# Merge stage of an encoder block: how the inverse row sums of the attention are read, and which engine issues the reads

## The reference, cut to what matters

```python
probs = p / (jnp.sum(p, axis=-1, keepdims=True) + jnp.exp(sink - m))      # branch A; branch B: softmax
ya = swa_gqa_sinks(...) @ w_o_a[l];  yb = chunk_relbias_attention(...) @ w_o_b[l]
gates = jax.nn.sigmoid(h @ w_branch_gate[l] + b_branch_gate[l]).reshape(b, s, N_BRANCHES, d)
mixed = gates[:, :, 0] * ya + gates[:, :, 1] * yb
x = x + mixed @ w_out[l]
h2 = rmsnorm(x, norm_ffn[l])
g_logits = jnp.dot(hf, w_rg) + b_rg;  e_logits = jnp.dot(hf, w_re) + b_re
```

## Time and profile before

| what | us |
|---|---|
| three timed runs | 2922.29, 2931.5, 2965.14 |
| their median | 2931.5 |
| the profiled execution, its own time | 2918.7 |
| its span, first to last instruction | 2917.1 |
| mean granted TensorE clock | 0.915 of full speed |
| TensorE busy with matmuls | 2510.5 (86% of the span) |
| VectorE, ScalarE, GpSimd busy | 1341.9, 1045.2, 702.0 |

### The profile page before, as it was taken

How to read it: one execution, slowest core, us unless ns; L and a number is a source line. 1 busy time by engine, 2 the same in 40 slices (tenths; PEclk the granted TensorE clock), 3 DMA queues, 4 the chain that set the end, 5 groups by cost and what they waited for, 6 DMA issues and landing times. The chain is left out here.

```text
span 2917.1 us, 37013 instructions
## 1 busy us (share of the span) xinstructions
PE 2510.5 (86%) x12254; PEld 2071.1 (71%) x12255; DVE 1341.9 (46%) x1962; ACT 1045.2 (36%) x1705; POOL 702.0 (24%) x693
## 2 busy tenths in 40 slices
PE   3899986899996999959389999947999999999950
PEld 3788865788884777748288888836888888888840
DVE  7101122100003666626433332256876767787958
ACT  4111111111113566624321111114654646666722
POOL 4264555500000000000022112102332323233342
PEclk9999998999996999959699998968999999999975
DMA  4245566761214544165553433336886868798968
GB/s 138 87 135 168 202 186 182 226 242 65 86 50 125 125 118 97 43 139 127 168 158 126 137 124 113 101 118 246 315 303 230 316 230 316 260 373 316 352 231 330
DMA packets 237631, 540.18 MB, mean 185 GB/s; under 512 B 55840, under 2 KB 90080, under 8 KB 232304
## 3 DMA queue, kind: packets, MB, share of 16 engines
q1 hardware_dynamic: 190160, 400.73, 41.7%
q0 software_dynamic: 27056, 89.67, 9.3%
q10 hardware_dynamic: 20336, 48.77, 4.6%
HBM read 405.07 MB, written 134.02 MB: 185 GB/s over the span
## 5 line engine op out<-in xcount | busy, mean ns | idle before, releaser
L394 DVE TENSOR_TENSOR pj_w_lo<-pj_w_raw,pj_w_hi 128x1024 fp32r<-128x1024 f32 x46 | 61.9, 1350 | 665.0 <-ACT pj_w_hi L333 664.7
L333 ACT ACTIVATE pj_w_hi<-pj_w_raw 128x1024 fp32r<-128x1024 f32 x46 | 48.6, 1059 | 640.2 <-PE pj_bank L436 525.1
L436 PE MATMUL pj_bank<-pj_hT_hi,pj_w_hi 128*128 128x512 f32 x960 | 257.6, 390 | 3.5 <-DVE pj_w_lo L394 3.5
L436 PE MATMUL pj_bank<-pj_hT_lo,pj_w_hi 128*128 128x512 f32 x960 | 257.4, 390 | 0.0
L436 PE MATMUL pj_bank<-pj_hT_hi,pj_w_lo 128*128 128x512 f32 x960 | 257.2, 390 | 0.0
L1767 POOL TENSOR_TENSOR ex_wd_lo<-weights_raw_d,ex_wd_hi 128x1024 fp32r<-128x1024 f32 x64 | 194.5, 3059 | 131.7 <-ACT ex_wd_hi L1792 131.7
L436 PEld LDWEIGHTS pj_bank<-pj_hT_hi,pj_w_hi 128*128 128x128 f32 x960 | 180.7, 188 | 41.3 <-DVE pj_w_lo L394 3.9
L436 PEld LDWEIGHTS pj_bank<-pj_hT_lo,pj_w_hi 128*128 128x128 f32 x960 | 180.8, 188 | 37.6
L436 PEld LDWEIGHTS pj_bank<-pj_hT_hi,pj_w_lo 128*128 128x128 f32 x960 | 180.8, 188 | 37.6
L1414 PE MATMUL mg_y_ps<-mg_aT_hi,mg_w_hi 128*128 128x256 f32 x512 | 156.2, 305 | 56.1 <-DVE mg_aT_lo L1326 49.0
L1857 DVE TENSOR_TENSOR ex_wd_lo<-weights_raw_d,ex_wd_hi 128x1024 fp32r<-128x1024 f32 x64 | 169.2, 2681 | 9.8 <-ACT ex_wd_hi L1792 9.8
(11 more groups left out here) (245 smaller groups left out, 5833.3 us busy)
## 6 DMA issues: line engine op xcount, KB each, us to landing
weights_raw_g<-in_w_exp_gate_dram SPq DMA_DIRECT2D x128, 512.0 KB
weights_raw_u<-in_w_exp_up_dram SPq DMA_DIRECT2D x128, 512.0 KB
weights_raw_d<-in_w_exp_down_dram SPq DMA_DIRECT2D x128, 512.0 KB
scratch_ys<-ex_y ACTq DMA_DIRECT2D x47, 512.0 KB, 4.4
pj_w_raw<-in_w_feat_dram SPq DMA_DIRECT2D x46, 512.0 KB, 5.9
scratch_gates<-pj_f_hi SPq DMA_DIRECT2D x32, 512.0 KB, 3.4
scratch_ys<-pj_g_row POOLq DMA_DIRECT2D x32, 512.0 KB, 16.2
mg_g_in<-scratch_gates SPq DMA_DIRECT2D x128, 128.0 KB, 2.9
```

What stands on the lines that cost most here:

```text
L333: act.activation(w_hi[n % 2][:], w_raw[n % 2][:], ACT.Copy).then_inc(whi_done, 1)
L394: dve.tensor_tensor(w_lo[n % 2][:], w_raw[n % 2][:], w_hi[n % 2][:], ALU.subtract).then_inc(wlo_done, 1)
L436: last = pe.matmul(eight[4 * p + b][:], w[p][:, k * P:(k + 1) * P], h[:, k, b * NB:(b + 1) * NB], start=(k == 0 and n == 0), stop=(k == KD ...
```

## The change

Seven edits, all in merge:

1. The two buffers inv_in go. All inverse sums of a block (128 partitions by 8 feature tiles by 256) are read into inv_all, which is the memory of aT_lo under another type.
2. GpSimd issues the reads, two for a block: one for the even heads, one for the odd, each 64 partitions by 8 rows of 1 KB.
3. In a block GpSimd makes all eight sums first, then waits for y_done of the whole block (aT_lo is free then), issues the two reads for the next block, and scales its eight tiles one after another.
4. ScalarE issues no inverse sums.
5. At the start GpSimd waits for the inversion, stores the inverses, and reads them back.
6. SyncE's order at the start is: row sums, slabs 0 to 3, attention block 0, slabs 4 to 8, the constants, the rest of the slabs.
7. VectorE waits for the constants after its splits, TensorE after its block 0.

```diff
-        inv_in = [st.sb(f"inv_in{p}", [P, MB]) for p in range(2)]
         aT_lo = st.sb("aT_lo", [P, KD, MB], F32R)
+        inv_all = aT_lo[:].bitcast(F32)
...
         def _(sp):
-            sp.dma_start(g_row[:], norm_ffn.partition_broadcast(P)).then_inc(const_in, 16)
-            sp.dma_start(idt[:], ident).then_inc(const_in, 16)
-            sp.dma_start(w_r[:], w_router.rearrange("p (k n) -> p k n", k=KD)).then_inc(const_in, 16)
-            sp.dma_start(b_r[:], b_router.partition_broadcast(P)).then_inc(const_in, 16)
...
             sp.dma_start(row_sum, sums[:2 * HEADS, :].rearrange("h (s n) -> (h s) n", n=MB)).then_inc(sums_in, 16)
             sp.dma_start(sink_row, sums[2 * HEADS:, :].rearrange("h (s n) -> (h s) n", n=MB)).then_inc(sums_in, 16)
-            load_att(0)
             for s in range(OUT_SLABS):
                 if s >= 4:
                     sp.wait_ge(w_lo_done, s - 3)
-                if s == 4:
-                    sp.wait_ge(inverted, 1)
-                    sp.dma_start(inv_rows.rearrange("h (s n) -> (h s) n", n=MB), row_sum).then_inc(inv_out, 16)
-                if s == 6:
-                    sp.wait_ge(inv_out, 16)
-                    load_inv(0, 0)
-                    load_inv(0, 1)
-                if 8 <= s < 8 + KD // 2 - 1:
-                    for k in range(2 * s - 14, 2 * s - 12):
-                        sp.wait_ge(att_scaled, k - 1)
-                        load_inv(0, k)
                 sp.dma_start(w_raw[s % 4][:], w_mix[s]).then_inc(w_in[s % 4], 16)
+                if s == 3:
+                    load_att(0)
+                if s == KD:
+                    sp.dma_start(idt[:], ident).then_inc(const_in, 16)
+                    sp.dma_start(w_r[:], w_router.rearrange("p (k n) -> p k n", k=KD)).then_inc(const_in, 16)
+                    sp.dma_start(b_r[:], b_router.partition_broadcast(P)).then_inc(const_in, 16)
+                    sp.dma_start(g_row[:], norm_ffn.partition_broadcast(P)).then_inc(const_in, 16)
...
         def _(pool):
+            def load_inv(i):
+                for half in range(2):
+                    pool.dma_start(inv_all[half * DH:(half + 1) * DH, :, :],
+                                   inv_rows.rearrange("(k s) n -> s k n", s=2)[half][:, ds(i * MB, MB)].partition_broadcast(DH)
+                                   ).then_inc(inv_ready, 16)
+
             def scale_att(i, k):
-                pool.wait_ge(att_ready, i * 16 + 16)
-                pool.wait_ge(inv_ready[k % 2], i * (KD * 16) + (k // 2 + 1) * 32)
-                pool.tensor_tensor(att_f[:, k, :], att_f[:, k, :], inv_in[k % 2][:], ALU.mult).then_inc(att_scaled, 1)
+                if k == 0:
+                    pool.wait_ge(att_ready, i * 16 + 16)
+                    pool.wait_ge(inv_ready, i * 32 + 32)
+                pool.tensor_tensor(att_f[:, k, :], att_f[:, k, :], inv_all[:, k, :], ALU.mult).then_inc(att_scaled, 1)
...
                     pool.tensor_tensor(mixed[o % 2], gated[o % 2][:, :MB], gated[o % 2][:, MB:],
                                        ALU.add).then_inc(mixed_done, 1)
-                    if more and o >= SCALE_STEP:
-                        scale_att(i + 1, o - SCALE_STEP)
                 if more:
-                    for k in range(KD - SCALE_STEP, KD):
+
+                    pool.wait_ge(y_done, i * KD + KD)
+                    hold(pool, held)
+                    load_inv(i + 1)
+                    for k in range(KD):
                         scale_att(i + 1, k)
 
+            pool.wait_ge(inverted, 1)
+            pool.dma_start(inv_rows.rearrange("h (s n) -> (h s) n", n=MB), row_sum).then_inc(inv_out, 16)
+            pool.wait_ge(inv_out, 16)
+            load_inv(0)
             for k in range(KD):
                 scale_att(0, k)
...
                     act.activation(mix_hi[:, o, :], mixed[o % 2], ACT.Copy).then_inc(mix_hi_done, 1)
-                    if more and o == 0:
-                        act.wait_ge(att_scaled, i * KD + KD)
-                        hold(act, held)
-                        for k in range(2):
-                            load_inv(i + 1, k)
-                    if more and o >= 2:
-
-                        act.wait_ge(att_scaled, i * KD + KD + o - 1)
-                        hold(act, held)
-                        load_inv(i + 1, o)
                     if behind and o in H_STEPS:
                         copy_h(i - 1, H_STEPS.index(o))
```

More of the change, by code:

```diff
@@ L1065, in __init__ @@
         self.last = st.sb("last", [1, EXPERTS], I32)
-SCALE_STEP = 2
 H_STEPS = (2, 4)
@@ L1108, in merge @@
         att_ready = st.sem("att_ready")
-        inv_ready = [st.sem(f"inv_ready{p}") for p in range(2)]
+        inv_ready = st.sem("inv_ready")
         att_scaled = st.sem("att_scaled")
@@ L1236, in split @@
                     act.activation(w_hi[:, s, :], w_raw[s % 4][:], ACT.Copy).then_inc(w_hi_done, 1)
[L1238 to L1242, removed]
             def att_hi(i, first=False):
@@ L1312, in split @@
                                       ALU.subtract).then_inc(w_lo_done, 1)
-            dve.wait_ge(const_in, 64)
             def invert():
@@ L1345, in _ @@
             split(KD)
+            dve.wait_ge(const_in, 64)
             def over_block(i, behind, more=True):
@@ L1386, in _ @@
             pe.sem_inc(logit_mm, 1)
-            pe.wait_ge(const_in, 64)
             pe.wait_ge(w_lo_done, KD)
@@ L1441, in _ @@
             over_block(0, False)
+            pe.wait_ge(const_in, 64)
             with pe.Fori(1, NBLK) as i:
```

## The result

| | us, median (lowest to highest, runs) |
|---|---|
| before | 2920.83 (2910.26 to 2965.14, 20) |
| after | 2930.38 (2924.20 to 2976.30, 20) |
| ratio | 1.0046, 95% interval 1.0031 to 1.0061 |

Predicted were 2878 us, with a range of 2858 to 2912. Measured is a small loss of 9 to 18 us by the interval. The medians are over all 20 runs, while every ratio here leaves out the few executions over 1.5% longer than the shortest of the same kernel (2976.30 us above is one, and in experiment 2 one of 6042.82 us that nothing here explains). The wait that the change was priced on did go. A new one took its place.

What follows compares the result with a forecast made beforehand. The prediction took TensorE's merge stalls behind ScalarE's copy, delayed by inverse-row loads, as the bound. -43.6 (y stages) - 10.4 (start) + 5.6 (new stall) = -48.4 us, from a usual 2926 us predicted as 2878 us, range 2858 to 2912.

Steps and rivals of the forecast that it cites:

- What bounds the kernel: Merge, y stages: TensorE waits 23.5 us for ScalarE's copy, delayed by inverse-row loads, and its clock falls in the stall.
- Part 1: Y stages of blocks 1 to 6: ScalarE issues no inverse rows, saving 43.6 us, priced by block 7, which loads none.
- Part 2: Out stage: one inverse-row load and one scaling chain per block, the new cost; landing at Y+8.3, last low part at Y+17.7.
- Y: The end of a block's y stage in the merge, from which the prediction counts times in us.
- The chain: Out stage: GpSimd's eight scalings and the parts behind them, put at 9.4 us if VectorE blocks GpSimd, 7.3 if not.
- Who is late: Out stage: late low parts delay VectorE's residual adds, the gate and TensorE's third column tile; 0.8 us a block, 5.6 us.
- The threshold of Y+16.9: Out stage: from E at Y+16.9, each later microsecond moves half 1's adds, the gate and TensorE's next third column tile.
- E: The end of a block's last low part on VectorE in the out stage, predicted at Y+17.7.
- the slow rival: Out stage: GpSimd's loads land late, E at Y+28.7, stall 11.8 us and 3 more at half clock; +50 us, 2976; chance 0.06.
- Part 3: Merge start: row sums first on SyncE, first y matmul near 1441 instead of 1451.37; gain 10.4 us, bounds 4 and 16.
- The sum: Whole kernel: -43.6 - 10.4 + 5.6 = -48.4 us, from a usual time of 2926 us to 2878 us.
- signs of "Wrong": Merge trace: landings past Y+11, TensorE's clock falling at the third tile, y stages still at 35 us would refute the forecast.

Runs made afterwards that it cites:

- experiment 2: The changed kernel with the block loads of inverse rows issued by SyncE, not GpSimd: 2920.52 us, ratio 1.0002 to the kernel before.
- experiment 1: The kernel before with only the small inverse-row loads issued by GpSimd, not ScalarE: 2868.54 us against 2918.52, ratio 0.9845.
- experiment 8: The changed kernel with a block's inverse rows in a line in DRAM and its loads issued by SyncE: 2863.76 us, ratio 0.9835 to the kernel before.
- experiment 7: The changed kernel with 64 bytes of padding per 1 KB piece, rows 17 KB apart: 2861.72 us against 2915.63 for the kernel before, ratio 0.9847.
- experiment 4: The changed kernel with inverse rows in a line in DRAM, still issued by GpSimd: 2868.16 us, ratio 0.9825 to the kernel before.
- experiment 3: The changed kernel with probe loads added at the merge's quiet end, on GpSimd, then SyncE: one half landed in 8.0 and 8.6 us, both in 13.2 and 13.5.

## Why the prediction was wrong

**What bounds the kernel, and Part 1: right.** The control by block 7 gave 43.6 us; the edit alone gave 42.3 (experiment 1). In the changed kernel the gain is there too, as the 0.2 us of waits on the copy, but covered by the new loss.

**The step that failed: the landing in Part 2.** "I take landing at Y+8.3: Y+3.1+4.2 and 1.0 for the second half queueing behind the first." The scalings, which wait for the load, began at Y+16.6 to Y+17.5 instead, so the landing was some 8 to 9 us later than this term. Two parts of it were wrong. The 4.2 us came from a store with as many pieces but other addresses, each piece written once; the load's half alone took 8.0. The 1.0 for the second half came from the 384 GB/s of the earlier trace rows, a load of 1024 different rows; with both on their way, the second took 13.2 from its own issue, 5.2 more and not 1.0. Neither row had the property that decides: one row copied to 64 partitions, 16 KB from the next. The 0.3 us of addressing per issue is shown by no run, and the second issue stood at Y+2.5, not Y+3.1; that error was small and on the other side. The upper bound (line 294's 16.2 us, Y+19.3) did hold the true value, and was given too little weight, because its reason (32 stores queueing) did not apply. What was missing was a row with the same read pattern; the small loads of before read only one row each and lacked the distance.

**The chain: 7.9 us, not 9.4.** From 1553.23 to 1561.1. The eight scalings took 6.47 us, where 5.84 + 2.1 = 7.9 had been put: they are hardly held up. It is VectorE's low parts that stretch, from 0.689 us in the earlier trace rows to a median of 1.088. The contention was foreseen, the side that pays was not. The Trainium skill, SBUF — State Buffer, section "Who interferes with whom", leaves it to the order of issue who waits; the prediction took it to be GpSimd. In this chain the trace shows the longer instruction at VectorE, with scalings at a median of 0.737 us. The 2.40 us of the earlier trace rows stood beside VectorE's splits.

**Who is late: right.** The threshold of Y+16.9 held from both sides. With E at Y+15.9 (experiment 8, block 1) half 1's adds waited for TensorE and y stages were 29.1 to 29.4 us; with E at Y+17.5 (experiment 7) they began 5.1 us behind half 0's and y stages were 29.4 to 31.5. For block 1 of the changed kernel the rule gives 25.4 - 16.9 = 8.5 us, and the third tile starts 8.4 us later than before, counted from Y. Over the seven blocks E is Y+25.0 on average, the rule gives 8.1, and the third tile is 7.6 to 8.4 us late, 8.1 on average. Idle time shows less of it, 6.7 us a block (22.0 and 24.8 over seven), since in several blocks the first two tiles themselves ran longer (clock 0.66 from 1621.92 to 1630.50). On top, the slow rival had 3 us a block for matmuls at half clock. What the whole lateness cost is seen in the stages, as seven gaps and the excess of the y stages over block 7's 29.2 us of before: out 175.7 - 152.5 = 23.2, y of 1 to 6 212.0 - 175.2 = 36.8, y of 7 5.4, together 65.4, or 9.3 per block, where the prediction had 0.8. Less 8.1 leaves 1.2 behind the third tile, where the clock is low (0.55 from 1571.79 to 1577.00).

**Part 3: 2.0 us, not 10.4.** The reciprocal came earlier by more than assumed: it ends at 1408.4, 4.9 us after SyncE's first issue, against 9.6 before. The load ate it up:

```profile
1408.69 0.54 POOL L1214 DMA_DIRECT2D scratch_inv_rows<-mg_hT  x1 [159.67 <-DVE mg_hT L1298]
1414.51 1.41 POOL L1188 DMA_DIRECT2D mg_aT_lo<-scratch_inv_rows  x2 [5.28 <-DMA scratch_inv_rows<-mg_hT]
1432.26 7.37 POOL L1196 TENSOR_TENSOR mg_att_f<-mg_att_f,mg_aT_lo 128x256 f32<-128x256 f32 x8 [16.34 <-DMA mg_aT_lo<-scratch_inv_rows]
```

17.75 us from its issue to the first scaling, where 7.2 had been put. With the quick layouts the start gained 6.9 to 8.6 us (32.7, 31.6 and 31.0 against 39.6). It was only in part the same failed term: with the rows 17 KB apart (experiment 7) the same stretch still took 13.1 us. So 4.6 us of the excess are the place of the rows; the other 5.9 remain there, and 2.5 with the rows in a line (experiment 4, 9.7 us). How much of that is the company of the slabs, for which "some 2" had been put, no run separates.

**The sum, mended.** -43.6 for Part 1, -2.0 for the start, +65.4 for the lateness, which the prediction had at +5.6, and +0.9 for the y stage of block 0 give +20.7 us; the merge measured +20.3. That they add up is bookkeeping, as the stages are cuts of the same merge. What tests the lateness is the rule (8.1 of the 9.3 us a block) and experiment 7, where it goes with the layout.

**The rivals.** The slower one named the right mechanism and place, a late landing, and the point from which it decides (E at Y+21.6, or 7.7 us a block): E was Y+25.4 and the loss 9.3 a block. Its size was too large, as it took the landing and the chain later (Y+28.7) and more time at half clock. A chance of 0.06 was too low for the one term of the sum that no row of before showed. All three signs of "Wrong" came: landings past Y+11, the clock low at the third tile, y stages at 35 us.

## What to carry to other kernels

Price a transfer by one measured with the same pattern of reading, not only the same bytes and pieces: here 512 KB landed in 5 or in 8 us by where the rows lay. When rows of memory are copied to many partitions (here 1 KB rows to 64), keep their distance off multiples of 8 KB, by padding or by laying them in a line. And before moving work to cure a stall, try the smallest edit that takes the cause away: another engine for the same issues gave 42.3 of the 43.6 us.

## What the runs showed of the hardware

- Loads that copy each row to 64 partitions: 7.5 to 8.6 us for 512 KB with rows at multiples of 8 KB, 4.8 to 5.7 otherwise; different rows at 16 KB are quick (4.7). The DMA engines look busy meanwhile (share 0.75 at 74 GB/s in the merge), while the same load alone on SyncE's queue shows a share of 0.38 at 70 GB/s (experiment 3, 1983.3 to 1990.8). So the share does not tell how much they move.
- GpSimd's scalings keep their pace beside VectorE's low parts (6.47 us for eight), while the low parts stretch from 0.69 us to 1.09 in the median and 1.25 at most.
- The issue below, on SyncE's queue, took 0.43 us before the change and with the rows 17 KB apart (experiment 7). While the slow load and the slabs ran it took 2.62 us:

```profile
1424.11 2.62 SPq L1150 DMA_DIRECT2D mg_b_r<-in_b_router_dram  x1
```
